# Stick-breaking attention with queries on the partitions: a VectorE scan along the keys in place of two-part triangular products on TensorE

## The reference, cut to what matters

```python
def stick_breaking(q, k, v):                 # A[t,s] = sigmoid(z_ts) * prod_{s<j<t} (1 - sigmoid(z_tj))
    ...
        z = jnp.einsum('bhqd,bshd->bhqs', qblk, kf)
        log_beta = jax.nn.log_sigmoid(z)
        log_1m = jnp.where(mask, log_beta - z, 0.0)          # = -softplus(z) where key < query
        cum = jnp.cumsum(log_1m, axis=-1)
        log_a = log_beta + cum[..., -1:] - cum               # a suffix sum over the keys after s
        a = jnp.where(mask, jnp.exp(log_a), 0.0)
        return jnp.einsum('bhqs,bshd->bqhd', a, vf)
```

## Time and profile before

| | before |
|---|---|
| median of 3 runs | 926.05 us |
| the profiled execution, by the clock of the runs | 925.98 us |
| its span, first to last instruction | 924.2 us |
| PE busy | 913.5 us (99%) |
| DVE busy | 591.6 us (64%) |
| ACT busy | 483.9 us (52%) |
| POOL busy | 44.4 us (5%) |
| mean granted clock of TensorE | 0.998 |

### The profile page before, as it was taken

One profiled execution on the slowest core, in us unless ns is written; L12 is line 12 of the kernel. 1 busy time (PEld: TensorE's weight loads), 2 busy tenths in 40 slices (PEclk: granted clock), 3 DMA queues, 4 the chain that ended last, 5 costly groups with the idle time before them and its releaser, 6 DMA issues.

```text
span 924.2 us, 13108 instructions
## 1 busy us (share of the span) xinstructions
PE 913.5 (99%) x5438; PEld 801.4 (87%) x5438; DVE 591.6 (64%) x637; ACT 483.9 (52%) x554; POOL 44.4 (5%) x79
## 2 busy tenths in 40 slices
PE   8999999999999999999999999999999999999997
PEld 7998998789998888888988888889978898888886
DVE  5565646567887545556577755558786677777643
ACT  6434787873445334434555534446854674555441
POOL 2010111110010000000000000001000010000000
PEclk9999999999999999999999999999999999999999
DMA  8666454444255655655466555546822385555651
GB/s 304 201 238 228 139 163 139 155 137 137 93 182 191 204 198 188 201 203 196 161 196 199 183 182 184 191 130 185 277 92 91 98 266 183 183 182 205 199 166 46
DMA packets 99531, 163.95 MB, mean 177 GB/s; under 512 B 4864, under 2 KB 37475, under 8 KB 99344
## 3 DMA queue, kind: packets, MB, share of 16 engines
q1 hardware_dynamic: 99472, 163.11, 53.8%
HBM read 162.03 MB, written 3.16 MB: 179 GB/s over the span
## 4 chain that ended last, share of the span: by engine, by line
PE 94%; DVE 3%; ACT 1%; issue 1%; DMA 1%; POOL 0%; SPq 0%; DVEq 0%; POOLq 0%; ACTq 0%
PE acc L540 14%; PE acc L541 14%; PE acc L542 14%; PE acc L548 8%; PE acc L550 7%; PE acc L552 7%; PE m L573 7%; PE acc L573 6%; PE m L578 4%; PE acc L578 3%; PE acc L589 1%; PE m L688 1%; DVE wlo L1458 1%; PE m L728 1%; PE acc L655 1%
## 5 line engine op out<-in xcount | busy, mean ns | idle before, releaser
L1458 DVE TENSOR_TENSOR wlo<-land,whi 128x2048 fp32r<-128x2048 f32 (+2 forms) x152 | 335.0, 2207 | 180.3 <-ACT whi L1043 180.1
L1043 ACT ACTIVATE whi<-land 128x2048 fp32r<-128x2048 f32 (+2 forms) x153 | 282.2, 1848 | 207.7 <-PE acc L542 146.0
L548 PE MATMUL acc<-xT,whi 128*128 128x256 f32 x592 | 170.4, 288 | 0.0
L550 PE MATMUL acc<-xT,whi 128*128 128x256 f32 x592 | 167.4, 283 | 0.0
L552 PE MATMUL acc<-xT,wlo 128*128 128x256 f32 x592 | 167.4, 283 | 0.0
L548 PEld LDWEIGHTS acc<-xT,whi 128*128 128x128 f32 x592 | 113.4, 192 | 3.6 <-issue 2.4
L550 PEld LDWEIGHTS acc<-xT,whi 128*128 128x128 f32 x592 | 113.5, 192 | 0.2
L552 PEld LDWEIGHTS acc<-xT,wlo 128*128 128x128 f32 x592 | 113.4, 192 | 0.0
L540 PE MATMUL acc<-whi,xT 128*128 128x512 f32 (+2 forms) x240 | 91.5, 381 | 0.0
L541 PE MATMUL acc<-wlo,xT 128*128 128x512 f32 (+2 forms) x240 | 90.3, 376 | 0.0
L542 PE MATMUL acc<-whi,xT 128*128 128x512 f32 (+2 forms) x240 | 90.1, 375 | 0.0
(11 more groups left out here) (400 smaller groups left out, 1372.9 us busy)
## 6 DMA issues: line engine op xcount, KB each, us to landing
land<-in_w_in SPq DMA_DIRECT2D x55, 1024.0 KB, 5.1
land<-in_w_up SPq DMA_DIRECT2D x16, 1024.0 KB, 5.2
land<-in_w_down SPq DMA_DIRECT2D x16, 1024.0 KB, 5.1
land<-in_w_ffn_gate SPq DMA_DIRECT2D x22, 512.0 KB, 4.0
land<-in_w_ffn_up SPq DMA_DIRECT2D x22, 512.0 KB, 5.1
land<-in_w_ffn_down SPq DMA_DIRECT2D x10, 1024.0 KB, 5.1
land<-in_w_in SPq DMA_DIRECT2D x14, 512.0 KB, 4.4
land<-in_w_out SPq DMA_DIRECT2D x6, 1024.0 KB, 5.1
```

The source lines that it names most:

```text
L548: mm(to, whi[:, s, k, cs], xh[:, k0 + k, :], start=first and c % 2 == 0, stop=False, skip_group_check=True)
L550: mm(to, whi[:, s, k, cs], xl[:, k0 + k, :], start=False, stop=False, skip_group_check=True)
L1043: activate(whi[:, u % PARTS, 0:m, 0:w], land[:, u % LANDS, 0:m, 0:w], ACT.Copy).then_inc(hi_ready, 1)
L1458: v.tensor_tensor(wlo[:, u % PARTS, 0:m, 0:w], land[:, u % LANDS, 0:m, 0:w], whi[:, u % PARTS, 0:m, 0:w].bitcast(F32), ALU.subtract).then_ ...
```

## The change

The scores are computed with the queries on the partitions and the keys along the free dimension; the triangular products go. A scan on DVE (`tensor_tensor_scan`, 128x384, restarted at column 128 by a zero in `carry`) sums the softplus along the keys, shifted by one element, and a second DVE operation subtracts that from z into `sba`. ACT's exponential takes the total as its bias (one instruction for the 128 columns of the first query tile and one for the 256 of the second). The weights now have the queries on the partitions, and PE transposes them, three 128x128 tiles for each head, before the value products; DVE copies the transposed tiles out of PSUM. ACT's exponentials move from odd i to even i, ahead of the exponential of mlo; the transposes stand in the middle of the odd unit; DVE's copies stand in odd i behind the weight split.

```diff
         def sb_scores(h):
-                mm(M[(h + i) % 4][:, 0:T], sbkT[hs, c, 0:P], sbqT[hs, c, :], start=True, stop=True)
+                mm(M[(h + i) % 4][:, P:3 * P], sbqT[hs, c, P:T], sbkT[hs, c, :], start=True, stop=True)
...
-                mm(M[(h + i) % 4][:, T:T + P], sbkT[hs, c, P:T], sbqT[hs, c, P:T], start=False, stop=True,
+                mm(M[(h + i) % 4][:, 0:P], sbqT[hs, c, 0:P], sbkT[hs, c, 0:P], start=False, stop=True,
...
-        def sb_remain(h):
-            pe.wait_ge(sb_lo, h + 1)
-            z = M[h % 4]
-            for w in (sbw_hi[:, h % 2], sbw_lo[:, h % 2]):
-                mm(z[:, 0:3 * P], sums_r[:, 0:P], w, start=False, stop=True, skip_group_check=True)
-                last = mm(z[:, P:T], sums_r[:, P:], w[:, T:3 * P], start=False, stop=True, skip_group_check=True)
-            last.then_inc(sb_r, 1)
+        def sb_turn(h):
+            pe.wait_ge(sb_am, h + 1)
+            for i in range(3):
+                last = nc.tensor.transpose(M[h % 4][:, i * P:(i + 1) * P], sba[:, h % 2, i * P:(i + 1) * P], ident)
+            last.then_inc(sb_at, 1)
...
         def sb_values(h):
-            pe.wait_ge(sb_am, h + 2)
+            pe.wait_ge(sb_ac, h + 2)
...
         def between(u, k):
+            if k == 2 and u - SB0 in range(3, SB_H + 2, 2):
+                sb_turn(u - SB0 - 3)
+                sb_turn(u - SB0 - 2)
...
-        def sb_leading(h):
-            act.wait_ge(sb_tm, h + 1)
-            if h >= 2:
-                act.wait_ge(sb_r, h - 1)
-            activate(sbw_hi[:, h % 2], sbw[:, h % 2], ACT.Copy).then_inc(sb_hi, 1)
-
         def sb_weights(h):
-            act.wait_ge(sb_r, h + 1)
-            if h >= 2:
-                act.wait_ge(sb_av, h // 2)
-            activate(sba[:, h % 2], M[h % 4][:, 0:3 * P], ACT.Exp).then_inc(sb_a, 1)
+            act.wait_ge(sb_d, h + 1)
+            w, c = sba[:, h % 2], sbc[:, h % 2]
+            activate(w[:, 0:P], w[:, 0:P], ACT.Exp, bias=c[:, P - 1:P])
+            activate(w[:, P:], w[:, P:], ACT.Exp, bias=c[:, 3 * P - 1:3 * P]).then_inc(sb_a, 1)
...
             if i % 2 == 0 and 2 <= i <= SB_H:
-                sb_leading(i - 2)
-                sb_leading(i - 1)
+                sb_weights(i - 2)
+                sb_weights(i - 1)
...
-            if i % 2 == 1 and 3 <= i <= SB_H + 1:
-                sb_weights(i - 3)
-                sb_weights(i - 2)
...
-        def sb_rest(h):
-            dve.wait_ge(sb_hi, h + 1)
-            v.tensor_tensor(sbw_lo[:, h % 2], sbw[:, h % 2], sbw_hi[:, h % 2].bitcast(F32),
-                            ALU.subtract).then_inc(sb_lo, 1)
+        def sb_scan(h):
...
+            dve.wait_ge(sb_tm, h + 1)
+            if h >= 2:
+                dve.wait_ge(sb_a, h - 1)
+                dve.wait_ge(sb_at, h - 1)
+            link(v.tensor_tensor_scan(sbc[:, h % 2], carry[:, :], sbw0[:, h % 2, 0:3 * P], 0.0, ALU.mult, ALU.subtract))
+            v.tensor_tensor(sba[:, h % 2], M[h % 4][:, 0:3 * P], sbc[:, h % 2], ALU.subtract).then_inc(sb_d, 1)
+
+        def sb_copy(h):
+            dve.wait_ge(sb_at, h + 1)
+            if h >= 2:
+                dve.wait_ge(sb_av, h // 2)
+            v.tensor_copy(sbaT[:, h % 2], M[h % 4][:, 0:3 * P]).then_inc(sb_ac, 1)
...
             if i % 2 == 0 and 2 <= i <= SB_H:
-                sb_rest(i - 2)
-                sb_rest(i - 1)
+                sb_scan(i - 2)
+                sb_scan(i - 1)
+            if i % 2 == 1 and 3 <= i <= SB_H + 1:
+                sb_copy(i - 3)
+                sb_copy(i - 2)
```

More of the change, by code:

```diff
@@ L247, in build @@
     early.close()
-    sbw_hi = sb("sbw_hi", [P, 2, 3 * P], F32R, stack=area)
-    sbw_lo = sb("sbw_lo", [P, 2, 3 * P], F32R, stack=area)
-    sums_r = sb("sums_r", [P, 2 * P], F32R, stack=area)
+    sbaT = sb("sbaT", [P, 2, 3 * P], stack=area)
+    sbc = sb("sbc", [P, 2, 3 * P], stack=area)
+    carry = sb("carry", [P, 3 * P], stack=area)
     area.close()
@@ L267, in build @@
     mlo = sb("mlo", [P, TT, D], stack=mix)
-    sbw = sb("sbw", [P, 2, 3 * P], stack=mix)
+    sbw0 = sb("sbw", [P, 2, 3 * P + 1], stack=mix)
+    sbw = sbw0[:, :, 1:]
     sba = sb("sba", [P, 2, 3 * P], stack=mix)
@@ L364, in build @@
     cols_turned, c_ready, floor_ready = sem("cols_turned"), sem("c_ready"), sem("floor_ready")
-    sums_ready, sb_hi, sb_lo = sem("sums_ready"), sem("sb_hi"), sem("sb_lo")
-    sb_z, sb_log, sb_t, sb_tm, sb_r, sb_a, sb_am, sb_av, sb_y = (
-        sem(n) for n in ("sb_z", "sb_log", "sb_t", "sb_tm", "sb_r", "sb_a", "sb_am", "sb_av", "sb_y"))
+    sb_d, sb_at, sb_ac, sb_set = sem("sb_d"), sem("sb_at"), sem("sb_ac"), sem("sb_set")
+    sb_z, sb_log, sb_t, sb_tm, sb_a, sb_am, sb_av, sb_y = (
+        sem(n) for n in ("sb_z", "sb_log", "sb_t", "sb_tm", "sb_a", "sb_am", "sb_av", "sb_y"))
     sb_y_hi = sem("sb_y_hi")
@@ L714, in sb_scores @@
                 hs = slice(SB_D * i, SB_D * (i + 1))
-                mm(M[(h + i) % 4][:, 0:T], sbkT[hs, c, 0:P], sbqT[hs, c, :], start=True, stop=True)
+                mm(M[(h + i) % 4][:, P:3 * P], sbqT[hs, c, P:T], sbkT[hs, c, :], start=True, stop=True)
             for i in range(2):
                 hs = slice(SB_D * i, SB_D * (i + 1))
-                mm(M[(h + i) % 4][:, T:T + P], sbkT[hs, c, P:T], sbqT[hs, c, P:T], start=False, stop=True,
+                mm(M[(h + i) % 4][:, 0:P], sbqT[hs, c, 0:P], sbkT[hs, c, 0:P], start=False, stop=True,
                    skip_group_check=True).then_inc(sb_z, 1)
-        def sb_remain(h):
-            if h == 0:
-                pe.wait_ge(sums_ready, 1)
-            pe.wait_ge(sb_lo, h + 1)
-            z = M[h % 4]
-            for w in (sbw_hi[:, h % 2], sbw_lo[:, h % 2]):
-                mm(z[:, 0:3 * P], sums_r[:, 0:P], w, start=False, stop=True, skip_group_check=True)
-                last = mm(z[:, P:T], sums_r[:, P:], w[:, T:3 * P], start=False, stop=True, skip_group_check=True)
-            last.then_inc(sb_r, 1)
+        def sb_turn(h):
[3 more added lines that the diff above has]
+            last.then_inc(sb_at, 1)
         def sb_values(h):
-            pe.wait_ge(sb_am, h + 2)
+            pe.wait_ge(sb_ac, h + 2)
             to = M[h % 4]
@@ L737, in sb_values @@
                 mm(to[SB_D * i:SB_D * (i + 1), 0:T], sbv[:, 0, (h + i) * SB_D:(h + i + 1) * SB_D],
-                   sba[:, i, 0:T], start=True, stop=False, skip_group_check=True)
+                   sbaT[:, i, 0:T], start=True, stop=False, skip_group_check=True)
             for i in range(2):
                 last = mm(to[SB_D * i:SB_D * (i + 1), P:T], sbv[:, 1, (h + i) * SB_D:(h + i + 1) * SB_D],
-                          sba[:, i, T:3 * P], start=False, stop=True, skip_group_check=True)
+                          sbaT[:, i, T:3 * P], start=False, stop=True, skip_group_check=True)
             last.then_inc(sb_av, 1)
@@ L998, in _ @@
             i = u - SB0
[L999 to L1004, removed]
+            if i % 2 == 0 and 0 <= i < SB_H:
+                sb_scores(i)
             if i % 2 == 1 and 3 <= i <= SB_H + 1:
@@ L1117, in sb_logs @@
                 if i >= 2:
-                    act.wait_ge(sb_lo, i - 1)
+                    act.wait_ge(sb_d, i - 1)
                 link(activate(sbw[:, i % 2], M[i % 4][:, 0:3 * P], ACT.Abs))
@@ L1512, in sb_softplus @@
                                    op1=ALU.add).then_inc(sb_t, 1)
-        def sb_rest(h):
-            dve.wait_ge(sb_hi, h + 1)
-            v.tensor_tensor(sbw_lo[:, h % 2], sbw[:, h % 2], sbw_hi[:, h % 2].bitcast(F32),
-                            ALU.subtract).then_inc(sb_lo, 1)
+        def sb_scan(h):
+            if h == 0:
+                dve.wait_ge(sb_set, 2)
+            dve.wait_ge(sb_tm, h + 1)
[9 more added lines that the diff above has]
+            v.tensor_copy(sbaT[:, h % 2], M[h % 4][:, 0:3 * P]).then_inc(sb_ac, 1)
         def sb_result(h):
@@ L1887, in _ @@
             i = u - SB0
-            if i % 2 == 0 and 2 <= i <= SB_H:
-                sb_rest(i - 2)
-                sb_rest(i - 1)
+            if i == 0:
+                dve.wait_ge(tab_out, 16)
+                v.memset(carry[:, :], 1.0)
+                v.memset(sbw0[:, :, 0:1], 0.0).then_inc(sb_set, 1)
+                dve.wait_ge(sb_set, 1)
+                v.memset(carry[:, P:P + 1], 0.0).then_inc(sb_set, 1)
+            if i % 2 == 0 and 2 <= i <= SB_H:
+                sb_scan(i - 2)
[3 more added lines that the diff above has]
+                sb_copy(i - 2)
             if i % 2 == 1 and 1 <= i < SB_H:
@@ L2125, in inverse_root, with keep @@
                                    ALU.pow), rstd_ready)
-        def keep(view, above):
+        def keep(view, above, free=1):
             w = view.rearrange("p (a c) -> p a c", c=P)[:, 0:3:2, :]
-            return g.affine_select(out=w, in_=w, pattern=[[0, 2], [1, P]], compare_op=above, fill=0.0, base=0,
-                                   channel_multiplier=-1)
```

(6 more changed lines are left out.)

## The result

The changed kernel takes 931.09 us (median of 4, 930.4 to 932.18), the kernel before 926.1 beside it: ratio 1.0049, 95% interval 1.0037 to 1.0062. It is slower by 0.5%, 5.0 us, where 2.8 were forecast.

The account below looks back on a forecast made before the run. PE was taken to bound the attention's stretch; 3.3 us of saved PE work against 6.1 us of waits from a 14.3 us ACT-DVE loop gave +2.8 us, 925.98 to 928.8 us, range 924.8 to 932.8.

Parts of the forecast that it names:

- The bound: Attention's stretch, 89 to 210 us: PE busy without a gap, so a microsecond of PE work removed is one won.
- What PE gains and pays: Each pair on PE: triangular products save 1.11 us, six transposes cost 0.70; over eight pairs PE's work falls 3.3 us.
- R: Start of ACT's result copy, once every two units; forecast to come about every 14.3 us after the change.
- The chain on ACT and DVE: DVE's split, scans, ACT's exponentials and odd split, DVE's copies: two loops of about 14.3 us against PE's 14.22 and 13.69.
- mlo and the gate: Late cycles: mlo's exponential adds 1.2 us to the loop, DVE's 3.84 us output gate delays the tail; PE waits 1.8 and 2.3.
- The sum: Pair by pair to the last value products: 3.3 us less PE work, 6.1 us of waits, so +2.8 us, 928.8 us.
- the clock: Rival: PE's clock falls at the new gaps or transposes, at least 5.8 us more, 934 us or above; chance 0.02.
- The bounds: Forecast case's range, 927.3 to 931.2 us, from 0.2 us either way in seven links and 1 us in the tail.
- The rule on transposes: The skill's rule that transposes aren't counted as PE activity: the 5.6 us of transposes would up to double; given 0.02.
- The forecast's likeliest case: PE's waits in the attention's stretch exceed its saved work: 927.3 to 931.2 us, chance 0.5.

Follow-up runs that it names:

- experiments 6 to 8: Changed kernel with DVE's scans ahead of its split (923.96 us); scans and copies ahead (922.82); these plus mlo's exponential first and output gates one unit later (923.03).
- experiment 11: Kernel before the change with six of the eight triangular matmuls of each pair left out: 921.03 us, ratio 0.9949.
- experiment 6: Changed kernel with DVE's two scans ahead of its weight split in even iterations, nothing else: 923.96 us, ratio 0.9971.
- experiment 5: Changed kernel with DVE's two copies of the transposed weights ahead of its weight split in odd iterations: 927.48 us, ratio 1.0012.
- experiment 10: Changed kernel with scans and copies ahead of DVE's splits, and each scan issued twice: 926.23 us, ratio 0.9995.
- experiment 9: Changed kernel with each scan issued twice: 946.3 us, ratio 1.0207.
- Experiment 3: Changed kernel with DVE's four output gates one unit later, mlo's exponential left in its place: 929.74 us, ratio 1.0029.
- experiment 4: Changed kernel with 18 unused matmuls into a free bank in PE's gap before the last value products: 929.06 us, ratio 1.0028.
- experiment 7: Changed kernel with both scans and copies ahead of DVE's splits: 922.82 us, ratio 0.9965.

## Why the prediction came out as it did

**The bound.** Right: PE was continuous, and where the loop allows it (experiments 6 to 8) saved PE work comes back one for one. It held only within the slack that experiment 11 shows, some 0.6 us in a token cycle.

**What PE gains and pays.** Right. Six transposes hold the stream 0.65 us (121.04 - 120.15 - 0.24), the lower bound and 0.05 under what I took. With them PE's own cycle is 14.63 - 1.11 + 0.65 = 14.17, which is exactly the R of experiment 6.

```profile
120.15 0.28 PE L553 MATMUL acc<-xT,wlo 128*128 128x256 f32 x1
120.27 0.82 PE L726 MATMUL m<-con,sba 128*128 128x128 f32 x6
120.84 0.36 PE L549 MATMUL acc<-xT,whi 128*128 128x256 f32 x1
121.04 0.28 PE L551 MATMUL acc<-xT,whi 128*128 128x256 f32 x1
```

**The chain on ACT and DVE.** Right in the terms that it has: scan 0.95 (0.96 taken), table load ahead of the wait, ACT's odd split 8.18 us after R (8.10), R every 14.30 to 14.34 (14.32). That two loops close at about the same length is shown too: opening the one left the other (experiment 5, at 14.22 and 14.33), shortening both freed PE (6). One thing in it is luck: the sum lets DVE's split wait for ACT's, while in token cycles DVE comes to it straight from softplus, evacuation and the result's rest (153.20 to 155.80, without a pause), 2.26 us after R where the sum has 2.23. This second condition was in no sum; here it costs nothing, in experiment 10 it was what I had left out. DVE's load was not the point, as 9 and 10 show: 15.7 us of DVE work cost 15.2 in the loop and 3.4 outside.

**mlo and the gate.** Right: 15.46 for the cycle with mlo (15.5); PE's wait 1.72 (1.8) and 2.29 (2.3). Experiment 3 adds what the sum only implied, that ACT's and DVE's delays in the tail run side by side.

**The sum.** Its terms up to the last value products are met within 0.1 us. The step that failed is the clock. It stood among the rivals with 0.02 and a price of 5.8 us, and as an alternative to the forecast; it belonged behind the forecast's own 2.3 us gap, as a term of the sum, with a price of 1.5. The prediction says that no row shows the lower level, and that holds for the rows it shows; the trace of before has it once, behind PE's last matmul, which ends at 918.55:

```profile
918.00:920.00 2.00, 0.55 (x3) 0.13 (x1) 0.60 (x1) 1.07 (x3) 0.00 (x0) 1.00 0.67 230
920.00:922.00 2.00, 0.00 (x0) 0.00 (x0) 1.76 (x5) 0.00 (x0) 0.00 (x0) 0.80 0.06 23
922.00:924.00 2.00, 0.00 (x0) 0.00 (x0) 0.00 (x0) 0.00 (x0) 0.00 (x0) 0.50 0.69 240
```

The level falls there with PE idle. No matmul follows, so the price could not be read, but a bound could have been: a few matmuls at double their slot. With 1.5 the sum is 4.3, and 0.4 of the rest is the start of this execution.

**The bounds.** The low end of the forecast is summed wrongly. 0.2 us in each of seven links and 1 us in the tail are 2.4 us either way: 926.4 to 931.2, not 927.3. Nothing else in the prediction hangs on it.

**The rule on transposes.** The prediction weighed it with 0.02. The Trainium skill, "TensorE: Matmul & The Clock Gate", Part 4, says that transposes don't count as activity for the clock. With eight groups of six between full streams the granted clock stays 1.00 here from 100 to 205 us in the changed kernel and through the whole stretch in experiments 6 to 8. In this placement the rule has no effect; the fall came behind idle time.

**The forecast's likeliest case** was the one that happened, with its mechanism; the measured 931.1 lies at the upper end of that case's own range because of the clock. That it is still inside is luck: the margin was made for the links and the tail, which needed 0.1 us of it, and the clock's 1.5 happened to fit.

## What to carry to other kernels

When steps alternate between engines that work their programs in order, write down the closed loop (who waits for whom until the first engine is back), add its terms, and compare it with the bounding engine's cycle: that, not the busy share, says what a change may add. Work inside the loop is paid in full, the same work a few lines earlier in the same program may be free: two pairs of calls moved in DVE's program turned a loss of 5 us into a gain of 3.5. And a gap of the matmul engine costs its length plus, at times, the matmuls behind it at half clock.

## What the runs showed of the hardware that I had not expected

The granted clock fell from 1.00 to 0.50 behind an idle time of 2.29 us of a PE that had been busy without a break for 13 us, and in two more kernels behind 2.2 us; not behind 0.9, 1.1, 1.3 or 1.7. In the profiled execution of experiment 9 it did not fall behind gaps of up to 2.4 us. So the length of the gap alone doesn't decide it.

Nor does it take a long gap. Two profiled executions have a fall in the second block, far from the change: that of experiment 4 at 696 to 700 us and that of experiment 7 here.

```profile
684.00:688.00 4.00, 3.21 (x25) 2.92 (x24) 3.77 (x11) 1.37 (x6) 0.00 (x0) 1.00 0.43 135
688.00:690.00 2.00, 1.96 (x13) 1.50 (x13) 0.18 (x1) 2.00 (x3) 0.00 (x0) 1.00 0.00 0
690.00:692.00 2.00, 2.00 (x11) 1.96 (x11) 2.00 (x1) 1.04 (x5) 0.00 (x0) 0.57 0.00 0
692.00:694.00 2.00, 2.00 (x12) 2.00 (x12) 1.90 (x8) 0.00 (x0) 0.00 (x0) 0.58 0.27 52
```

From 670 us up to this fall PE had only two waits, 0.36 us that ended at 682.76 and 0.82 at 688.04, ahead of small matmuls. The same two stand in the profiles of the changed kernel and of the one before, at 1.00. The sixteen matmuls from 690.44 to 693.79 take 3.35 us for 1.92, 1.4 us more; this execution took 924.55 us where the other four took 922.67 to 922.83.

This may be much of the scatter of all kernels. Eleven of the 56 executions of the kernel before that stood beside the experiments took 927.2 to 927.9 us, the others 925.9 to 926.7, which suits a fall of this kind without any gap of the change. A single time 1.5 us up therefore doesn't say which fall it had. What decides whether the clock falls was not settled: only one execution of each kernel was profiled.
